# Another order of the granule buffers in SBUF, and three expert loads issued elsewhere in SyncE's stream

## The reference

```
h = rms_norm(x, norm1_w)
x = x + mixer(h @ w_in) @ w_out       # 12 heads: FoX attention, retention, gated delta rule
h = rms_norm(x, norm2_w)
g   = argmax over 4 groups of softmax(h @ rg_w + rg_b)
e   = top 2 of the 8 experts in g, weights normalised, times the group's probability
x = x + sum over the 2 chosen experts: (silu(h @ w1[e]) * (h @ w3[e]) * weight) @ w2[e]
out = rms_norm(x, final_norm_w)
```

## Time and profile before

| | before |
|---|---|
| median of 3 runs | 652.58 us (649.79 to 652.78) |
| profiled execution: its time | 648.96 us |
| profiled execution: its span | 647.0 us |
| TensorE busy | 570.8 us (88%) |
| VectorE, ScalarE, GpSimd busy | 250.0, 198.3, 169.6 us |
| moved by DMA | 151.62 MB, mean 234 GB/s |
| expert loads | 48 of 2048 KB, median 28.1 us from issue to landing |

### The profile page before, as it was taken

How to read it: one execution, slowest core, us unless ns; L and a number is a source line. 1 busy time by engine, 2 the same in 40 slices (tenths; PEclk the granted TensorE clock), 3 DMA queues, 4 the chain that set the end, 5 groups by cost and what they waited for, 6 DMA issues and landing times.

```text
span 647.0 us, 11786 instructions
## 1 busy us (share of the span) xinstructions
PE 570.8 (88%) x4816; PEld 441.8 (68%) x4816; DVE 250.0 (39%) x630; ACT 198.3 (31%) x429; POOL 169.6 (26%) x112
## 2 busy tenths in 40 slices
PE   2999999999998999999999946999999988777782
PEld 1997877799998888767779935666566555444430
DVE  4316453582215522467762163323323332221127
ACT  5445435532333162434535330112111111111113
POOL 1344334172358322300124201111121111101003
PEclk9999999999999999999999975999999999999996
DMA  8556893422122111000079977999999999999984
GB/s 315 180 183 195 49 217 93 131 67 67 39 62 66 34 37 64 1 2 2 1 232 408 379 279 307 422 415 420 418 420 420 419 418 420 419 421 418 418 322 192
DMA packets 51989, 151.62 MB, mean 234 GB/s; under 512 B 12527, under 2 KB 31775, under 8 KB 39392
## 3 DMA queue, kind: packets, MB, share of 16 engines
q1 hardware_dynamic: 47312, 142.69, 60.0%
q0 software_dynamic: 4560, 8.15, 3.4%
q10 hardware_dynamic: 64, 0.02, 0.0%
HBM read 142.70 MB, written 16.27 MB: 246 GB/s over the span
## 4 chain that ended last, share of the span: by engine, by line
PE 56%; SPq 14%; DMA 11%; DVE 8%; POOL 5%; issue 4%; ACT 2%; ACTq 0%; POOLq 0%; DVEq 0%
PE bank L706 24%; PE bank L730 7%; PE bank L988 5%; SPq L603 5%; DMA w<-in_expert_w_dram 4%; PE bank L1023 4%; PE bank L1003 4%; SPq L600 4%; DMA raw<-in_w_in_dram 4%; SPq L606 3%; POOL wlo L1315 2%; PE bank L958 2%; PE bank L972 2%; PE bank L864 1%; DMA yt<-yd 1%
## 5 line engine op out<-in xcount | busy, mean ns | idle before, releaser
L1315 POOL TENSOR_TENSOR wlo<-raw,whi 128x1024 fp32r<-128x1024 f32 (+1 forms) x38 | 91.0, 2397 | 181.2 <-ACT whi L1044 181.2
L706 PE MATMUL bank<-whi,hHi 128*128 128x256 f32 (+2 forms) x320 | 96.2, 301 | 2.7 <-DVE cacc L1475 1.4
L706 PE MATMUL bank<-wlo,hHi 128*128 128x256 f32 (+2 forms) x320 | 93.7, 293 | 0.0
L706 PE MATMUL bank<-whi,hLo 128*128 128x256 f32 (+2 forms) x320 | 93.6, 293 | 0.0
L1044 ACT ACTIVATE whi<-raw 128x1024 fp32r<-128x1024 f32 (+1 forms) x38 | 40.3, 1060 | 97.7 <-PE bank L706 86.1
L988 PE MATMUL bank<-w,xT 128*64 128x256 f32 x512 | 60.5, 390 | 10.5 <-issue 7.5
L1003 PE MATMUL bank<-w,xT 128*64 128x256 f32 x512 | 58.3, 380 | 6.7 <-DMA w<-in_expert_w_dram 6.7
L988 PEld LDWEIGHTS bank<-w,xT 128*64 128x64 f32 x512 | 39.4, 141 | 36.4 <-issue 20.5
L706 PEld LDWEIGHTS bank<-whi,hHi 128*128 128x128 f32 x320 | 60.2, 188 | 5.7 <-DVE hLo L1720 2.1
L1023 PE MATMUL bank<-w,hidT 128*64 128x512 f32 x256 | 58.5, 598 | 4.2 <-ACT hidT L1292 2.5
L706 PEld LDWEIGHTS bank<-whi,hLo 128*128 128x128 f32 x320 | 60.2, 188 | 1.4
(11 more groups left out here) (322 smaller groups left out, 884.6 us busy)
## 6 DMA issues: line engine op xcount, KB each, us to landing
w<-in_expert_w_dram SPq DMA_DIRECT2D x48, 2048.0 KB, 28.1
raw<-in_w_in_dram SPq DMA_DIRECT2D x24, 512.0 KB, 4.2
yd<-zt SPq DMA_DIRECT2D x8, 512.0 KB, 5.2
raw<-in_w_out_dram SPq DMA_DIRECT2D x8, 512.0 KB, 4.1
yt<-yd SPq DMA_DIRECT2D x4, 1024.0 KB, 9.2
raw<-in_w_in_dram SPq DMA_DIRECT2D x6, 520.0 KB, 7.2
X<-in_x_dram SPq DMA_DIRECT2D x4, 512.0 KB, 6.4
x<-in_x_dram SPq DMA_DIRECT2D x4, 512.0 KB, 5.9
```

The lines of the kernel that those rows point to most:

```text
L706: m = pe.matmul(o, l, r, start=(at == 0 and c == 0 and i == 0), stop=(at == parts - 1 and kc == chunks[-1] and i == 2), skip_group_check=True)
L1315: pool.tensor_tensor(part(wlo[g % 2], g), part(raw[g % 3], g), part(whi[g % 2], g).bitcast(F32), ALU.subtract).then_inc(wlo_done, 1)
```

## The change

The buffers of the last granule (`raw[1]`, `whi[1]`, `wlo[1]`) now come first, in the 12,480 bytes from 49 KB on; whi0, raw2, raw0 and wlo0 follow in this order. With it w2[1] (from 65 KB on) lies over buffers that granule 36 or an earlier one is the last to use, and over none of granule 37. SyncE now issues w2 of unit 1 before the third write to `h2d`, as soon as TensorE has read granule 36. w2 of unit 2 follows w3 of unit 2, and neither it nor w1 of unit 3 waits for the gather of unit 0 any more.

```diff
-        raw = [at(f"raw{i}", [P, HK, WMAX], R2 + i * gsz) for i in range(3)]
-        whi = [at(f"whi{i}", [P, HK, WMAX], R2 + (3 + i) * gsz, F32R) for i in range(2)]
-        wlo = [at(f"wlo{i}", [P, HK, WMAX], R2 + (5 + i) * gsz, F32R) for i in range(2)]
+        late = (GR - 1) % 3, (GR - 1) % 2
+        raw = [at(f"raw{i}", [P, HK, WMAX], R2 + (0 if i == late[0] else 3 + (i - late[0]) % 3) * gsz) for i in range(3)]
+        whi = [at(f"whi{i}", [P, HK, WMAX], R2 + (1 if i == late[1] else 3) * gsz, F32R) for i in range(2)]
+        wlo = [at(f"wlo{i}", [P, HK, WMAX], R2 + (2 if i == late[1] else 6) * gsz, F32R) for i in range(2)]
+        assert 3 * gsz <= 16 * KB
...
             for n in range(NOUT):
+                if n == NOUT - 1:
+                    sp.wait_ge(half_used, PART_DONE[GR - 2])
+                    load_w2(1)
                 for t in range(T):
                     wait_read(sp, ("y", NIN + n, t))
                 cs = slice(OUTB[n][0], sum(OUTB[n]))
                 sp.dma_start(h2d.ap().rearrange("(t p) d -> p t d", p=P)[:, :, cs], x2[:, :, cs]).then_inc(s_h2d, 16)
             sp.wait_ge(slots_freed, 3)
-            load_w2(1)
             load_w1(2)
             load_w3(2)
+            load_w2(2)
             sp.wait_ge(s_h2d, 16 * NOUT)
             sp.wait_ge(ssp_done, 1)
             wait_read(sp, ("hT", KC - 2))
             wait_read(sp, ("hT", KC - 1))
-            sp.wait_ge(gathered[0], 16)
-            load_w2(2)
             load_w1(3)
```

## The result

The changed kernel takes 654.62 us (median of 20 runs, 652.14 to 659.09); the kernel before, run beside it, 652.39 us (20 runs). The ratio, which leaves out one slow run of before at 680.63 us, is 1.0047, with a 95% interval of 1.003 to 1.0064: 3.1 us slower (the plain quotient of the two medians is 1.0034, or 2.2 us). In a second series of 12 runs the ratio was 1.0024 (0.9996 to 1.0052). The profiled execution after has a span of 654.4 us.

A forecast was written before the change was run, and what follows sets the result against it. TensorE was taken to set the pace for eight units, then DMA, whose 48 loads set the end. 2.3 us gained and 2.3 given back left the 652.6 us median, own range 649 to 654, full range 648.3 to 656.5.

The forecast's parts named there:

- the two terms that were to cancel: DMA behind the first gather gains 2.3 us; unit 0's gate matmuls ending later give 2.3 us back.
- the rival in which the first gather takes the place of the wait: First gather lands at 402.5 us, 5.1 later, clock costs 1.1: 3.9 us slower, 656.5 us; chance 0.16.
- Both gaps: DMA's idle stretches at 371.2 to 376.3 and about 394.6 to 398.0 us, some 8 us together, were to close.
- the ten buffers are full before gate 0 ends: Loads fill all buffers at 399.5 us; the next waits for unit 0's gate matmuls, leaving DMA empty to 407.2 + d.
- The rival of 10 us gained: Two loads move in formerly idle DMA time and nothing idles later: 10.0 us faster, 642.6 us; chance 0.08.
- The layout is worth nothing by itself: The new order of granule buffers costs no time: same shapes, read and written by the same instructions.
- The rival that the change does not do what it says: w2 of unit 1 goes out no sooner, say because SyncE's queue is full: 652.6 us again; chance 0.05.
- The gather under load: First gather, with loads in flight, takes 8.4 us where it took 5.9, landing at 399.7 us.
- d: How much later unit 0's gate matmuls end because of the first gather: taken as 2.3 us, between 0 and 5.1.
- The rival without a late gather: First gather is not delayed by the loads, being small with its own queue: 2.3 us faster, 650.3 us; chance 0.17.
- The gain of 2.3 us that was to pay for it: From the eleventh load to w1 of unit 5 landing, less DMA work and overhead: 1.6 to 2.9 us gained, before d.
- The check that a load is in hand whenever the next one comes: DMA is still busy when each load issued at 411.03 to 429.36 us, shifted by d, arrives.

The follow-up runs named there:

- before kept busy: Kernel before plus 88 transposes of the identity, result unread, in TensorE's stream during the routing, against the kernel before; ratio 0.9986 (0.9961 to 1.001).
- the last, busier kernel: Changed kernel with w1 of unit 3 waiting for the first gather and 135 transposes in TensorE's waits; ratio to before 0.9972 (0.9949 to 0.9995).
- the kernel before with its gate late: Kernel before plus four idle ScalarE copies ahead of unit 0's gate matmuls, against the kernel before; ratio 1.0046 (1.0018 to 1.0073).
- the late gate in the changed kernel: Changed kernel plus four idle ScalarE copies ahead of unit 0's gate matmuls; ratio to the kernel before 1.0103 (1.007 to 1.0136).
- the other busier kernel: Changed kernel plus 135 transposes of the identity in TensorE's waits up to unit 0's gate matmuls; ratio to before 1.0023 (0.9997 to 1.005).

## Why the prediction was right, and where it was off

The measured 654.62 us lies in the full range (648.3 to 656.5), 2.0 above the 652.6 forecast and outside the 649 to 654 that the forecast gave for itself. "No change" with 0.69 was right by its bound of 0.5%, but only just, at 1.0047, and that is luck: the two terms that were to cancel were both off to the same side, and the interval of the ratio excludes 1. The kernel is slower, by a good part of the way to the rival in which the first gather takes the place of the wait (656.5 us). That rival was to decide once gate 0 ended after 408.7 us, with the gather landing after 399.7; on before's clock they came at 409.4 and 400.2. It was right in its sign, not in its size: the gather was 3.0 us late, not 5.1, and the clock cost nothing. Point by point:

- **Both gaps close, and the ten buffers are full before gate 0 ends.** Right but for one slow row (148 GB/s at 377), which cost nothing: w2 of unit 1 at 367.4 on before's clock, DMA empty of loads from 401, the eleventh load issued at the end of gate 0. The rival of 10 us gained is ruled out by this wait.
- **The layout is worth nothing by itself.** Right within the interval (0.9993, 0.9961 to 1.0025). The rival that the change does not do what it says is ruled out for w2 of unit 1, which moved; and since the kernel with only the wait removed lost as much, its price would have been the same.
- **The gather under load, 8.4 us, d = 2.3.** Right in kind, a little small: 8.9 and 9.0 us, and gate 0 3.0 us later (18.13 for 15.12). The clock followed the gate matmuls at no cost of its own (5.79 and 5.68 us for 5.81), as taken. The rival without a late gather is ruled out; only in kernels with one load or both behind the gather did it stay under 6.3 us.
- **The gain of 2.3 us that was to pay for it.** This step failed. It said that from the eleventh load to the landing of w1 of unit 5 the overhead would be 1.1 to 2.4 us. It was: landing 434.72 + 16.5 = 451.2, less the restart 0.8 us after 411.4, is 39.0 us, of which 33.8 are loads, gathers and scatters, so 5.2 us, where 1.7 were taken. DMA starts slowly from nothing (115 and 246 GB/s in two rows, 1.1 us, where the lower end allowed no slow start). Then it falls to 328 and 188 GB/s at 426 to 428, just after the scatter and the gather of units 0 and 3 are issued (424.24 and 425.56 us) and before any of their bytes move (from 429): 1.5 us lost in the 20 us, for 0.1 in before. About 1 us of the excess stays unexplained. The check that a load is in hand whenever the next one comes held; that DMA then moves at 420 GB/s did not.
- **The dip is not this execution's alone, and its cause is open.** Counted in the same way, the 20 us from 24 us behind the gather's issue on lose 0.1 to 0.4 us in before, in before kept busy and in the layout alone, 0.5 in the last, busier kernel, and 1.0 to 1.5 in all the others, the kernel before with its gate late among them. In the changed kernel only w2 of unit 3 was outstanding from 425.7 to 428.7, but in before it was alone too, from about 421.8 to 423.7, at 451 GB/s in 422:423; so a short queue by itself does not explain it.

With d = 3.0 the sum put the landing of w1 of unit 5 0.7 us later than in before, counted from the gather's issue; it came 4.3 us later (58.0 for 53.7). By the time of the runs, 3.1 us, it should have read: nothing gained, 3.0 us given back. Directly shown are that the wait for the gather is the edit that costs (three executions without it, 57.8 to 58.1 us; 53.0 to 54.0 in four kernels with it and nothing else added) and that a gather that is not late takes the cost away. That it acts by way of gate 0's end is supported by the late gate in the changed kernel and by the busier one, each with one profile. Whether the kernel before has any time in hand there stays open, and so does how the two executions of the changed kernel, with equal gate ends and w1 of unit 5 within 0.2 us, came to differ by 1.4 us at the last w3.

The Trainium skill (DMA: Bandwidth & Descriptors, Issuing engines are not separate DMA queues) has the direction right: all transfers share the 16 engines, and the gather was slower under load. As a mere taking of turns I had priced it at 0.7 us from that page, an estimate; the gather cost 3 us, so the measurement stands. The Trainium skill's fit for a transfer started by GpSimd (the same page, Anatomy of one DMA), 2.0 us and the bytes at 436 GB/s, would by estimate give 2.7 us for the gather's 0.3 MB; alone it took 3.9 and 4.0 us here.

## What to carry to other kernels

An idle stretch ahead of a phase bound by transfers is worth something only if there is a free buffer for every load that would fill it; otherwise it moves to behind the last buffer, and what counts is when the first buffer comes free again. Before removing a wait between bulk loads and a small transfer that the next work needs, ask what the small one costs under load: here 3 us on a gather of 0.3 MB outweighed 4 MB of loads that went out earlier. And the rate just after a restart is not the steady rate: 115 and 246 GB/s in two rows here, and 389 for 419 over 20 us a little later.

## What was not expected of the hardware

- The gather of unit 0 took 3.9 us with DMA idle (that of unit 1 4.0 to 4.1 us where the loads had just ended), 4.9 to 6.2 us when the load traffic ended on the way, and 8.7 to 9.4 us under full load. How much stood ahead made no difference there: by the rates some 3 MB of loads in the changed kernel and 5 MB in the one with only the wait gone, 8.9 and 9.0 us.
- The granted clock can fall while TensorE shows as busy. In the busier kernel in which w1 of unit 3 waits for the gather, TensorE was busy 0.51 and 0.75 of the two rows from 380 to 382 us and wholly from 382 on, first with the router's matmuls and from 384.0 with transposes. The clock was at half from about 383.2 to 386.6, and came back while TensorE ran nothing but transposes; in the other busier kernel, with the same two idle stretches ahead (0.72 and 0.25 us), it did not fall here. A row of the first:

```profile
384.00:385.00 1.00, 1.00 (x6) 1.00 (x7) 0.74 (x4) 0.00 (x0) 0.00 (x0) 0.50 1.00 410
```
